# GpSimd writes a weight unit's low part one step later in the second mixer, behind the next step's divisions

## The reference

```
def mixer_fox_nsa(h, w_in, b_f, cmp_pe, cmp_w1, cmp_w2, w_out):
    proj = h @ w_in                      # 1024 x 2840, padded to 23 units of 128 columns
    ...
    o_fox = fox_attention(fq, fk, fv, log_f)          # 8 heads, forget gates, causal
    ...
    o_nsa = nsa_attention(nq, kc, vc, ks, vs, kw, vw, gates, ...)
    return concatenate([o_fox, o_nsa]) @ w_out

# inside both attentions, for a block of 128 queries and a head
    p = masked_softmax(s, mask)          # exp(s - max), divided by its sum
    o = p @ v
# nsa: the selected and the windowed branch, each times its gate
```

## Time and profile before

| | |
|---|---|
| median of 3 runs | 1709.12 us (1707.95 to 1710.07) |
| the profiled execution's own time | 1709.2 us |
| its span in the trace | 1707.5 us, granted TensorE clock 0.991 of full speed |
| TensorE busy | 1647.5 us, 96% of the span |
| VectorE, ScalarE, GpSimd busy | 872.5, 707.0, 180.9 us |

### The profile page before, as it was taken

One profiled execution on the slowest core, in us unless ns is written; L12 is line 12 of the kernel. 1 busy time (PEld: TensorE's weight loads), 2 busy tenths in 40 slices (PEclk: granted clock), 3 DMA queues, 4 the chain that ended last, 5 costly groups with the idle time before them and its releaser, 6 DMA issues.

```text
span 1707.5 us, 22270 instructions
## 1 busy us (share of the span) xinstructions
PE 1647.5 (96%) x8099; PEld 1352.2 (79%) x8099; DVE 872.5 (51%) x1416; ACT 707.0 (41%) x1172; POOL 180.9 (11%) x246
## 2 busy tenths in 40 slices
PE   8999999999999999999889999999999999999996
PEld 6666788888878887888777888888888788888885
DVE  4543557777743336666656444443227644444223
ACT  4445454444432225676656332233225633333222
POOL 2011000000000022554522000002000200000000
PEclk9999999999999999999999999999999999999998
DMA  5211132333333262121112233333332133333331
GB/s 176 74 50 38 62 98 89 97 98 98 98 99 91 95 150 63 40 73 50 50 38 87 87 98 98 98 92 94 98 99 61 50 95 93 96 98 97 100 99 49
DMA packets 56005, 145.91 MB, mean 85 GB/s; under 512 B 14032, under 2 KB 18800, under 8 KB 55680
## 3 DMA queue, kind: packets, MB, share of 16 engines
q1 hardware_dynamic: 54528, 141.58, 26.8%
q0 software_dynamic: 688, 2.31, 0.6%
q10 hardware_dynamic: 720, 1.10, 0.2%
HBM read 139.72 MB, written 2.10 MB: 83 GB/s over the span
## 4 chain that ended last, share of the span: by engine, by line
PE 89%; ACT 3%; DVE 3%; POOL 2%; issue 1%; DMA 1%; SPq 0%; ACTq 0%; DVEq 0%
PE ps L1736 26%; PE ps L1738 26%; PE ps L1737 26%; POOL wlo L698 1%; ACT whi L745 1%; PE ps L1867 1%; PE ps L2123 1%; PE ps L2161 1%; PE ps L2108 1%; PE ps L2109 1%; PE ps L1857 1%; POOL pB L684 1%; DVE wlo L1176 1%; DMA raw<-w_in_a 1%; PE ps L1920 0%
## 5 line engine op out<-in xcount | busy, mean ns | idle before, releaser
L1736 PE MATMUL ps<-hhi,whi 128*128 128x512 f32 x1400 | 554.1, 396 | 7.5 <-DVE wlo L1176 4.8
L1738 PE MATMUL ps<-hhi,wlo 128*128 128x512 f32 x1400 | 547.7, 391 | 0.0
L1737 PE MATMUL ps<-hlo,whi 128*128 128x512 f32 x1400 | 547.7, 391 | 0.0
L1176 DVE TENSOR_TENSOR wlo<-raw,whi 128x1024 fp32r<-128x1024 f32 x238 | 291.5, 1225 | 497.8 <-ACT whi L745 495.1
L745 ACT ACTIVATE whi<-raw 128x1024 fp32r<-128x1024 f32 x251 | 265.5, 1058 | 583.3 <-PE ps L1738 581.4
L1736 PEld LDWEIGHTS ps<-hhi,whi 128*128 128x128 f32 x1400 | 264.2, 189 | 72.0 <-issue 7.5
L1738 PEld LDWEIGHTS ps<-hhi,wlo 128*128 128x128 f32 x1400 | 264.1, 189 | 55.7
L1737 PEld LDWEIGHTS ps<-hlo,whi 128*128 128x128 f32 x1400 | 264.2, 189 | 53.8 <-issue 1.2
L1736 PE MATMUL ps<-ahi,whi 128*128 128x512 f32 x528 | 205.5, 389 | 1.9 <-DVE wlo L1176 1.9
L1737 PE MATMUL ps<-alo,whi 128*128 128x512 f32 x528 | 205.4, 389 | 0.0
L1738 PE MATMUL ps<-ahi,wlo 128*128 128x512 f32 x528 | 205.4, 389 | 0.0
(11 more groups left out here) (327 smaller groups left out, 1792.5 us busy)
## 6 DMA issues: line engine op xcount, KB each, us to landing
raw<-w_up_b SPq DMA_DIRECT2D x88, 512.0 KB, 3.4
raw<-w_up_a SPq DMA_DIRECT2D x44, 512.0 KB, 3.4
raw<-w_in_b SPq DMA_DIRECT2D x23, 512.0 KB, 3.6
raw<-w_in_a SPq DMA_DIRECT2D x19, 512.0 KB, 3.5
raw<-w_down_b SPq DMA_DIRECT2D x16, 512.0 KB, 3.5
raw<-w_out_a SPq DMA_DIRECT2D x8, 512.0 KB, 3.5
raw<-w_down_a SPq DMA_DIRECT2D x8, 512.0 KB, 3.4
raw<-w_out_b SPq DMA_DIRECT2D x8, 512.0 KB, 3.5
```

Source lines behind the costliest of these rows:

```text
L1176: dve.tensor_tensor(wlow(n), raw[n % RAW][:, :], whigh(n).bitcast(f32), ALU.subtract).then_inc(lo_done, 1)
L1736: pe_.matmul(out, wh, hi, start=start, stop=False)
L1737: pe_.matmul(out, wh, lo, start=False, stop=False)
L1738: return pe_.matmul(out, wl, hi, start=False, stop=stop)
```

## The change

GpSimd's inner loop in step k runs over the units that were finished in step k - 1 instead of those of step k. Nothing else differs:

```diff
@@ -690,7 +690,7 @@
                         if k == nsa_at(t) + 3:
                             pool.wait_ge(B["cmp"], 5 * t + 5)
                             pool.tensor_tensor(pg, pg, over_keys(cst[:, 8:16]), ALU.mult).then_inc(B["cmp_pool"], 1)
-                    for u in finished_at("in_b", k):
+                    for u in finished_at("in_b", k - 1) if k else []:
                         n = mix_unit + u + 2
                         pool.wait_ge(hi_done, n + 1)
```

## The result

| | before | after |
|---|---|---|
| median of 14 runs each | 1709.47 us (1707.6 to 1719.32) | 1701.62 us (1699.2 to 1707.48) |
| ratio | | 0.9946, 95% interval 0.9933 to 0.9959 |
| span of the profiled execution | 1707.5 us | 1700.7 us |
| the mixer's stretch | 206.20 us | 199.22 us |

By the ratio the kernel is 0.54% faster; the two medians are 7.85 us apart, which is 0.46% and lies inside the interval. 1702.0 us was forecast. Single executions of one kernel differ by some microseconds, and the longer ones have the lower granted clock: 0.992 in the changed kernel's shortest run of 1699.2 us, 0.987 in its longest of 1707.48. For the experiments I therefore use a local measure, **the mixer's stretch**: from the start of the first matmul of unit 11 to the start of the first one of unit 25 (the third of `out_b`), which is the 336th behind it in the order of the weight matmuls.

The account below looks back on a forecast made before the run. TensorE, busy 1647.5 of 1707.5 us, waits for GpSimd divisions standing behind low parts. Terms 4.8 + 2.0 + 0.8 + 0.3 - 0.4 - 0.4 = 7.1 us off the 1709.12 median give 1702.0 us; range 1699.2 to 1705.7.

Parts of the forecast that it names:

- Pairs 13, 25, 37: TensorE's transposes no longer wait for divisions; scores then wait 0.18 us for VectorE's maximum; gain 1.61 us each, 4.8 together.
- Pairs 10, 22, 34: Transposes no longer wait for divisions and the maximum is early; gain 0.66 us each, 2.0 together.
- 3: Pair 3: its transposes no longer wait for divisions behind a low part; gain 0.8 us.
- 6, 18, 30: Pairs whose transposes exceed by about 0.1 us each behind a low part; gain 0.3 us together.
- Interference at 16 and 28: Steps 17 and 29: the low part holds up VectorE's conversions, delaying maximum and scores; loss 0.2 us each, 0.4 together.
- rival 1: No interference between low part and conversions on a long overlap; sum 9.0 us, time 1700.2 us; chance 15%.
- Pair 40: Step 41: the low part delays VectorE's conversions and maximum, so the 3.07 us excess isn't gained; loss 0.4 us.
- rival 3: TensorE's granted clock falls after standing still in step 42, costing about 3 us; time 1705 us; chance 10%.
- something that would prove me wrong: Sign against the forecast: a new TensorE wait for `wlo` or a swap, or PEclk below 1.00 between 840 and 880.
- The cover of the swaps: Step 41: key-half swaps start 1.1 us later behind SyncE's load, yet land 0.9 us before the scores of 851.68.

Follow-up runs that it names:

- the one-input experiment: Changed kernel with VectorE's conversions of fk1 to fk3 as a one-input scaling by 1, high-part subtraction left out; stretch 198.47 us, one run of 1701.08 us.
- the second experiment: Kernel before with only the low parts of units 15, 19 and 23 (ahead of pairs 13, 25, 37) moved; 1707.01 us, ratio 0.9982.
- the first experiment: Changed kernel, but low parts of units 16, 20 and 24 wait for VectorE's two key-unit conversions; stretch 202.84 us, median 1703.61 us, ratio 0.9957 to before.
- the best version: Changed kernel with those three low parts behind the conversions, fk1 to fk3 swaps ahead of the load, and two-operation L680 division; 1698.73 us, ratio 0.9921 to before.

## Why the prediction was right, step by step

- **Pairs 13, 25, 37** (1.61 each, 4.8): 1.53, 1.52 and 1.50, so 4.55. The maximum took over where I said, and costs 0.26 (1.79 - 1.53) instead of 0.18 us.
- **Pairs 10, 22, 34** (2.0), **3** (0.8) and **6, 18, 30** (0.3): 2.0, 0.8 and 0.27. I had missed 0.12 us at pair 14 and 0.14 at pair 26.
- **Interference at 16 and 28** (loss 0.4): 0.23 and 0.27. L1530's longest is 1.75 us, rival 1 said 0.69. The release is 0.14 us ahead of the low part's recorded end, as read from L721.
- **Pair 40** (loss 0.4): pair 42 is 0.36 later. From the conversions' start to the maximum, the record of the earlier trace rows stood at 846.87 - 843.77 = 3.10; it is 840.36 - 836.61 = 3.75 now, 0.65 later where 0.68 was said, and the exponential 0.37 later where 0.4 was said. With the low part out of the way the place gains 0.57, against 0.4 by my sum.
- **The clock.** Half of rival 3 came true: the granted clock did fall in step 42, which I had put at 10% and named as something that would prove me wrong.

```profile
840.00:842.00 2.00, 1.74 (x5) 1.04 (x6) 1.99 (x6) 1.53 (x5) 1.25 (x2) 0.73 0.94 301
842.00:844.00 2.00, 2.00 (x10) 1.81 (x9) 1.39 (x3) 1.95 (x4) 0.00 (x0) 0.50 0.29 84
844.00:846.00 2.00, 1.91 (x13) 1.55 (x13) 2.00 (x7) 1.78 (x5) 1.52 (x2) 0.91 0.00 0
```

  It cost next to nothing: in the one-input experiment the clock stayed at 1.00 there, the conversions took 0.52 us less (1.92), and pairs 40 and 42 stood 0.50 us closer (9.88 against 10.38), so that nothing is left over for the clock. The reason is argued: the exponential and the maxima of that step run on ScalarE and VectorE, and TensorE would have waited for them at full clock too. My price of 3 us for a fall held only for work that nothing covers, as in the second experiment (1.63).
- **The cover of the swaps** (0.9 us, "the thinnest cover") was reckoned for the wrong swap: the scores at 851.68 want the first half, which is issued 1.3 us sooner, so the cover was about 2 us: in the changed kernel that half landed at 842.92 and its scores start at 844.89. But the landing time isn't fixed: 3.5 to 4.1 us in step 42 of the changed kernel, up to 6.2 in the first experiment. The cover held; a swap 1.0 us later that also landed later broke it.

The sum was right to 0.1 us for the stretch with errors of either sign: 0.3 too much at 13, 25 and 37, 0.3 missed at 14 and 26, 0.1 too little for the losses. That they cancel to 0.1 is luck, and so is a median within 0.4 us of the forecast, since the changed kernel's single runs spread over 8 us.

## What to carry to other kernels

Of a step that is moved, follow every queue that waits for it, not only the engine that uses it: the best order on GpSimd paid only when SyncE's swaps no longer stood behind a load that waited for the same step. Measure a small change between two fixed points of the program instead of over the span, where falls of the clock add some microseconds in one execution and not in the next, and look for such falls between the two points as well. Where two runs lose the same time at the same place, read what the next engine waited for before calling it one cause.

## What the runs showed of the hardware

- GpSimd's low part holds up a one-input VectorE instruction too (0.42 us for 64x512 alone, 1.47 to 1.49 beside the low part). With two SBUF inputs on VectorE the holder was whichever began: the low part held L1530 here, and VectorE's L1176 held GpSimd's L721 in the earlier trace rows.
- A VectorE instruction with one of its two inputs in PSUM was not held: `ptl<-ps,pth` ran from 785.90 to 786.45 in the best version, wholly inside a low part, and took its usual 0.55 us.
- It depends on GpSimd's form too. The division with one operation did not hold up a conversion with two SBUF inputs that lay wholly inside it, three times in the changed kernel. In the first row the second division alone runs from 703.37 to 704.94 (128x512, 1.56 us):

```profile
702.15 2.79 POOL L680 TENSOR_SCALAR pB<-pB,fcB 128x384 f32<-128x384 f32 x2 [4.16 <-DVE fcB L1606]
...
703.96 0.69 DVE L1530 SCALAR_TENSOR_TENSOR qst<-zb,qst 64x512 fp32r<-64x512 f32 x1 [0.83 <-ACT qst L1026]
```

  With two operations (0.77) it does collide, in the best version; 1.20 and 0.87 us where 0.77 and 0.69 are free:

```profile
861.73 0.87 DVE L1683 TENSOR_TENSOR hlo<-outf,hhi 128x512 fp32r<-128x512 f32 x1
862.04 1.20 POOL L680 TENSOR_SCALAR sq<-sq,fcB,invc 128x512 f32<-128x512 f32 x1
```

  Why the one-operation form is half as fast and leaves VectorE alone stays open.
- A 128 KB swap landed in 2.2 to 2.4 us ahead of a 512 KB load, in 3.4 to 4.1 right behind it in the changed kernel, and in up to 6.2 in the first experiment.
